# Delta rule projections: both middle taps and the next high part ahead of the silus, the low part between convolution and scaling

## What is computed

```python
proj = h @ w_in
aq, ak, av, dqkv, dz, dab = jnp.split(proj, ...)
qkv = lax.conv_general_dilated(qkv_raw, conv_w[:, None, :], window_strides=(1,),
                               padding=[(2, 2)], feature_group_count=3 * DN_WIDTH)
qkv = jax.nn.silu(qkv)
q, k, v = jnp.split(qkv.reshape(b_, s_, 3, DN_HEADS, DN_HEAD_DIM), 3, axis=2)
q = l2_norm(q[:, :, 0]) * (DN_HEAD_DIM ** -0.5)
k = l2_norm(k[:, :, 0])
```

## Time and profile before

| | |
|---|---|
| three runs | 2824.68, 2827.41 (median), 2828.14 us |
| profiled execution | 2829.09 us, its span 2827.3 us |
| granted clock of TensorE, mean | 0.863 of full |
| busy: TensorE, weight loads | 2301.2 us (81%), 1686.2 us (60%) |
| busy: VectorE, ScalarE, GpSimd | 1194.7 us (42%), 850.7 us (30%), 190.0 us (7%) |
| stretch that the change touches | 1770 to 1866 us after the span's start |

### The profile page before, as it was taken

The page is one execution under the profiler, slowest core; times in us unless marked ns, Lnnn a source line. Parts: engine busy times, 40 slices in busy tenths (PEclk is TensorE's granted clock), DMA queues, the critical chain, the costliest instruction groups (busy, mean ns, idle before and its releaser), DMA issues. The chain is left out here.

```text
span 2827.3 us, 32605 instructions
## 1 busy us (share of the span) xinstructions
PE 2301.2 (81%) x13804; PEld 1686.2 (60%) x13804; DVE 1194.7 (42%) x1868; ACT 850.7 (30%) x1267; POOL 190.0 (7%) x190
## 2 busy tenths in 40 slices
PE   7889999959964577778999979877688588888784
PEld 5768888837832566557888857656676433333331
DVE  4336664374248454546665341654524411111112
ACT  4324443265242122334443244454103211010000
POOL 0000000000004111000000000000230011111100
PEclk9889999979986666789999989995858699999997
DMA  4112222212200001122222223120104199999996
GB/s 184 60 60 77 102 91 94 91 67 90 105 0 4 13 17 15 33 91 74 104 91 90 98 79 115 72 60 6 19 1 199 54 407 419 415 406 400 404 397 234
DMA packets 106597, 377.27 MB, mean 133 GB/s; under 512 B 54960, under 2 KB 55744, under 8 KB 67536
## 3 DMA queue, kind: packets, MB, share of 16 engines
q1 hardware_dynamic: 84848, 296.44, 28.4%
q10 hardware_dynamic: 9216, 67.11, 5.8%
q0 software_dynamic: 12384, 11.58, 1.4%
HBM read 375.31 MB, written 27.53 MB: 142 GB/s over the span
## 5 line engine op out<-in xcount | busy, mean ns | idle before, releaser
L582 PE MATMUL ps<-xh,wh 128*128 128x512 f32 x1384 | 556.0, 402 | 97.5 <-DVE wl L548 46.1
L583 PE MATMUL ps<-xl,wh 128*128 128x512 f32 x1384 | 551.0, 398 | 0.0
L584 PE MATMUL ps<-xh,wl 128*128 128x512 f32 x1384 | 549.4, 397 | 0.0
L548 DVE TENSOR_TENSOR wl<-raw,wh 128x2048 fp32r<-128x2048 f32 (+2 forms) x127 | 264.5, 2083 | 339.1 <-ACT wh L542 339.1
L582 PEld LDWEIGHTS ps<-xh,wh 128*128 128x128 f32 x1384 | 267.6, 193 | 172.5 <-issue 55.2
L3012 PE MATMUL ps<-egu,XT 128*64 128x512 f32 x1088 | 272.8, 659 | 84.2 <-DMA egu<-e_up 81.3
L584 PEld LDWEIGHTS ps<-xh,wl 128*128 128x128 f32 x1384 | 267.4, 193 | 57.5
L583 PEld LDWEIGHTS ps<-xl,wh 128*128 128x128 f32 x1384 | 268.0, 194 | 54.7
L542 ACT ACTIVATE wh<-raw 128x2048 fp32r<-128x2048 f32 (+2 forms) x127 | 220.2, 1735 | 82.6 <-PE ps L867 69.2
L3012 PEld LDWEIGHTS ps<-egu,XT 128*64 128x64 f32 x1088 | 94.5, 151 | 239.1 <-issue 228.2
L3030 DVE TENSOR_TENSOR HIDT<-ps,SIL 128x256 f32<-128x256 f32 x34 | 14.4, 425 | 350.6 <-ACT SIL L3022 350.6
(11 more groups left out here) (488 smaller groups left out, 3352.6 us busy)
## 6 DMA issues: line engine op xcount, KB each, us to landing
egu<-e_gate SPq DMA_DIRECT2D x68, 1024.0 KB, 14.8
egu<-e_up SPq DMA_DIRECT2D x68, 1024.0 KB, 25.0
ed<-e_down ACTq DMA_DIRECT2D x64, 1024.0 KB, 10.9
raw<-up SPq DMA_DIRECT2D x44, 1024.0 KB, 4.8
raw<-down SPq DMA_DIRECT2D x32, 704.0 KB, 4.0
raw<-rwkv_rkv SPq DMA_DIRECT2D x12, 1024.0 KB, 4.8
raw<-in_dn SPq DMA_DIRECT2D x8, 1024.0 KB, 4.9
raw<-sgu_u SPq DMA_DIRECT2D x4, 1024.0 KB, 8.4
```

The lines of the kernel that those rows point to most:

```text
L548: e.tensor_tensor(K.WL[s][:, 0:n], K.RAW[r][:, 0:n], K.WH[s][:, 0:n].bitcast(F32), SUB).then_inc(*K.w_low.mark(i))
L582: e.matmul(o, h[:, q, k], x_high[:, k], start=k == 0, stop=False)
L583: e.matmul(o, h[:, q, k], x_low[:, k], start=False, stop=False)
L584: last = e.matmul(o, l[:, q, k], x_high[:, k], start=False, stop=k == KT - 1)
```

## The change

On ScalarE the loop over m becomes a loop over the six items: the middle taps of both tiles, the high part of the next item, and then silu and square of both tiles. The small work that followed m = 4 now follows m = 5. On VectorE the low part moves from the start of an item's two tiles to a place between the convolution of the odd tile and the scaling of the attention's tile. Instructions and waits are otherwise the same.

```diff
+    def features(m):
+        dst = of_kq(K, m) if m < 8 else K.DV[:, m - 8]
+        e.wait_ge(*K.conv("in2_dn", m, 3))
+        if m >= 8:
+            e.wait_ge(*K.normed("sq_qk", m - 8))
+        e.activation(dst, K.T[m % 5], ACT.Silu).then_inc(*K.act_out.mark("in2_dn", m))
+        if m < 8:
+            e.wait_ge(*K.act_out("in2_dn", m))
+            e.activation(square_room(K, "sq_kq", m), of_kq(K, m), ACT.Square).then_inc(*K.square.mark("sq_kq", m))
+
+    def middle_tap(m):
         u = dn_use(K, m)
         e.wait_ge(*K.gemm_sum("in2_dn", m))
...
+    next_high(K, e, K.first["in2_dn"])
+    for i in range(6):
+        middle_tap(2 * i)
+        middle_tap(2 * i + 1)
+        next_high(K, e, K.first["in2_dn"] + i + 1)
+        features(2 * i)
+        features(2 * i + 1)
+        if i == 2:
...
-    next_high(K, e, K.first["in2_dn"] + 6)
...
+    next_low(K, e, K.first["in2_dn"])
     for m in range(12):
-        if m % 2 == 0:
-            next_low(K, e, K.first["in2_dn"] + m // 2)
...
         K.board.empty(u, K.conv("in2_dn", m, 3))
+        if m % 2:
+            next_low(K, e, K.first["in2_dn"] + m // 2 + 1)
         if m < 8:
...
-    next_low(K, e, K.first["in2_dn"] + 6)
```

More of the change, by code:

```diff
@@ L1961, in layer2_act @@
     next_high(K, e, K.first["in2_ab"])
-    for m in range(12):
-        if m % 2 == 0:
-            next_high(K, e, K.first["in2_dn"] + m // 2)
+    def features(m):
[8 more added lines that the diff above has]
+    def middle_tap(m):
         u = dn_use(K, m)
         e.wait_ge(*K.gemm_sum("in2_dn", m))
-        z = K.T[m % 5]
         if m < 5:
@@ L1971, in layer2_act @@
             e.wait_ge(*K.act_out("in2_dn", m - 5))
[L1972 to L1981, removed]
+        e.activation(K.T[m % 5], K.ps[:, u % 8], ACT.Copy, scale=K.prm("dncw", 24 + m)).then_inc(*K.act_out.mark("in2_dn", m, "tap"))
+    next_high(K, e, K.first["in2_dn"])
[6 more added lines that the diff above has]
+        if i == 2:
             e.wait_ge(*K.dve_delta("abs"))
```

## The result

The changed kernel has a median of 2810.49 us in four executions (2808.87 to 2818.14), beside 2827.54 us before: a ratio of 0.9946, 95% interval 0.9929 to 0.9963. The forecast was 2809.7 in a range of 2805 to 2817. The profiled execution took 2818.14 us with a span of 2816.4, the longest of the first four, so its end has to be read apart from its middle.

The account below looks back on a forecast made before the run. The engines' ping-pong between ScalarE and VectorE, not TensorE, was taken to set the pace of the delta rule's projections. Savings of 13.6 and 4.1 us, 17.7 together, taken from the median 2827.41 gave 2809.7 us, range 2805 to 2817.

Parts of the forecast that it names:

- Term one: Delta rule's projections, weight items 1 to 5: without the four waits the squares start at 1826.05, not 1839.68, saving 13.6 us.
- Term two: From the squares to weight item 6: the way falls from 13.41 to 9.34 us, saving 4.1 us.
- The slacks of blocks 1 and 3: Time to spare in the passes over tiles 2, 3 and 6, 7: 0.78 and 0.63 us, against 1.66 elsewhere.
- tap 6's delay: ScalarE behind block 2 (tiles 4, 5): two table loads for beta make tap 6 start 1.0 us later than otherwise.
- The reading that item 6 waits for the first logarithm: Weight item 6 needs the bank that the factors' first logarithm empties; it would start at 1835.39.
- The open cost at the squares: TensorE's 1.9 us pause before weight item 6 may bring 2.15 us of half clock: gain 17.7 with it, 19.9 without.
- The rows by which I chose between them: TensorE's earlier pauses: no half clock after 0.73 us, some after 2.28; 1.9 being nearer 2.28, the 2.15 us cost stayed in.
- Behind item 6 nothing differs: Stages after weight item 6, attention to experts: each waits on the one before, so all start 17.7 us earlier.
- the way to a slower kernel: Rival, attention and delta stretch: TensorE's clock falls low, up to 60 us more; at 45% of it 2836.7 us; chance 0.02.
- VectorE's slack: Rival, projections: VectorE's time to spare runs out in a block or two, one or two pauses, 2811 to 2816; chance 0.17.
- transfer of a later stage: Rival, later stages: a transfer set by a fixed time gives part of the gain back, 2816 to 2823; chance 0.04.

Follow-up runs that it names:

- a1_again: The changed kernel with no edit, twelve more executions in a later session and a second profile: 2812.86 us, ratio 0.9948 to the kernel before.
- a4_taps: The changed kernel with the high part put back behind the silus and squares, both middle taps still side by side: 2820.07 us.
- a5_high: The changed kernel with the odd tile's tap put back behind the even tile's silu and square, the high part ahead of them: 2817.10 us.
- f5_after_both: The changed kernel plus products of constants in TensorE's pauses in attention and ahead of the recurrence, to hold its clock: 2760.58 us.
- a2_scalar: The changed kernel with VectorE's low part put back behind the odd tile's scaling, so only ScalarE's order is new: 2815.78 us.

## Why the prediction was right, and where it was not

*The sum.* Term one was 13.6 us and measured 13.67 (68.22 less 54.55). Term two was 4.1 and measured 4.03. The slacks of blocks 1 and 3 were right to 0.1 us, tap 6's delay too (it starts at 1804.76). The reading that item 6 waits for the first logarithm, and not for the low part that the trace named, was right: after the change the profile names the logarithm, and in every profile of the table item 6 follows it.

*The open cost at the squares.* The pause was 1.84 us, forecast 1.9. In the profile of after, item 6 took 12.62 us with half clock in it, in that of a1_again 11.00 without. So the way from item 1 to attention is 18.1 or 19.7 us shorter than before, where the text had 17.7 and 19.9. Both ends occur. The Trainium skill ("TensorE: Matmul & The Clock Gate", Part 1: The HAM clock gate) states that the number of cold matmuls varies from run to run; these two profiles agree.

*The rows by which I chose between them were a bad guide.* I took the length of the pause (none after 0.73, half clock after 2.28) as what decides. The pause of 2.44 us in a4_taps had no half clock behind it, nor had the 2.00 in a5_high, and the same 1.84 had it once and once not.

*The step that failed* is "Behind item 6 nothing differs". The instructions don't, but the clock does. Attention took 90.9 to 99.4 us by profile, for the same work. I had this mechanism only as the way to a slower kernel, with 0.02, and argued against it by the three runs of before lying within 3.5 us. Three were too few: 5 of the 61 executions of that kernel on record lie some 21 us below the rest. The one profile of before has the long stretch at full clock; those of the changed order and its variants have it in some and not in others (a1_again and a4_taps have it). It cost 8.3 us in the profiled execution. In the medians the gain was 17.0 us in one session and 14.2 in the other, against 19.1 with that clock held, so some 2 to 5 us on average. The forecast of 2809.7 came near partly by luck, because the change gave up to 2 us more than its sum ahead of attention, and lost as much or more in it.

*The rivals.* VectorE's slack held in each block. That the high part runs beside the convolution cost nothing that can be seen. No transfer of a later stage held the gain back: in f5_after_both all of it arrives.

What stays open: why the clock falls 7 us into attention in one execution and about 23 us in another of the same program, and why the changed order meets the shorter stretch at full clock more often than the one before. That it does so rests on the medians and on one profile of the kernel before, not on a count of profiles.

## What to carry to other kernels

Where an in-order engine makes the next weights and also finishes the last results, put what needs only the finished sum (taps, high part) ahead of what waits for another engine; the cost of a wait there is that of everything queued behind it. Work the slack of each block out from start-to-start times, small instructions and table loads included, since the blocks with the least decide. And when a change shifts a stage of small matmuls, its gain isn't settled before TensorE's clock there is: hold it with products into an unused bank in the pauses, and compare both orders so.

## What the runs showed of the hardware

The granted clock of small matmuls was worth more than the change. At half clock the first five recurrence steps of the kernel before left TensorE no idle time for 45.6 us, and the clock stayed at 0.50 all the same, and through the last three steps with their pauses of 1.21 us. Only the profile of a2_scalar shows it rise in these steps, 27 us after their start. Ahead of the pause of 9.55 us the clock was at 1.00 in small matmuls too, of 64 to 128 columns (from 2010 to 2048.7). With 22 dense passes in that pause (9.71 us) the clock did not fall, and the steps kept it, with pauses of 0.64 to 1.21 us between them. Attention kept it with 1, 2 or 4 dense products in each pause. The Trainium skill ("TensorE: Matmul & The Clock Gate", HAM oscillation — how this bites in real kernels) describes a kernel in which the wait between short groups of matmuls makes each next group start cold; the fall in the pause of 4.36 us agrees. That the clock also fell behind a pause of 1.46 us, and that five steps without a pause stayed at half clock, stands in these profiles beside it.
